# Two projection stages in one block, with handed-on weight space and split rows kept in DRAM

## What is computed

```
h = rmsnorm(x, norm_mix_pre)
z = h @ w_in                                   # 1024 -> 3584 columns
rq, rk, rv, rg, dq, dk, dv = jnp.split(z, cuts, axis=-1)     # 7 x 512 columns
rq, rk = rope(rq), rope(rk) * RET_DK ** -0.5
ro, new_ret_state = retention_scan(ret_state, rq, rk, rv, block_len)   # 4 heads, chunk by chunk
ret_out = silu(rg) * rms_normalize(ro, NORM_EPS)
dq, dk = rope(dq), rope(dk)
do = diff_attention_core(dq, k_all, v_all, mask, lam, diff_subln, lambda_init)
mix = concatenate([ret_out, diff_out]) @ w_out
x = x + rmsnorm(mix, norm_mix_post)            # then a squared-ReLU MLP in the same manner
```

## Time and profile before

| | us |
|---|---|
| median of 3 runs (lowest, highest) | 2991.37 (2988.84, 2992.09) |
| the profiled execution, device time | 2985.41 |
| its span from first to last instruction | 2983.3 |
| PE busy | 2866.2 (96%) |
| DVE, ACT, POOL busy | 1461.7 (49%), 912.0 (31%), 276.8 (9%) |
| mean granted TensorE clock, as a share of 2.4 GHz | 0.982 |

### The profile page before, as it was taken

The page is one execution under the profiler, slowest core; times in us unless marked ns, Lnnn a source line. Parts: engine busy times, 40 slices in busy tenths (PEclk is TensorE's granted clock), DMA queues, the critical chain, the costliest instruction groups (busy, mean ns, idle before and its releaser), DMA issues.

```text
span 2983.3 us, 39174 instructions
## 1 busy us (share of the span) xinstructions
PE 2866.2 (96%) x14917; PEld 2347.8 (79%) x14917; DVE 1461.7 (49%) x2971; ACT 912.0 (31%) x1870; POOL 276.8 (9%) x413
## 2 busy tenths in 40 slices
PE   6999997999978999999889999999989999999998
PEld 5888886777856777766768888888878888988987
DVE  4322333423236887777544454454475445444455
ACT  3221222322125666666422112112133221211222
POOL 1111211111112111110000000000013000000001
PEclk9999998999979999999999999999999999999999
DMA  4101102433432211110321111111123111111113
GB/s 165 35 25 36 36 22 92 145 113 112 145 112 86 82 61 57 52 35 33 110 99 54 45 42 56 42 43 56 42 94 135 43 43 42 50 49 42 42 50 123
DMA packets 105887, 204.67 MB, mean 69 GB/s; under 512 B 11248, under 2 KB 48112, under 8 KB 105776
## 3 DMA queue, kind: packets, MB, share of 16 engines
q1 hardware_dynamic: 103472, 194.79, 19.8%
q0 software_dynamic: 2304, 8.39, 0.8%
HBM read 168.28 MB, written 34.87 MB: 68 GB/s over the span
## 4 chain that ended last, share of the span: by engine, by line
PE 65%; DVE 3%; ACT 1%; DMA 1%; issue 1%; POOL 0%; POOLq 0%; SPq 0%; DVEq 0%; ACTq 0%
PE bank L2191 24%; PE bank L2229 22%; PE bank L1514 6%; PE bank L1486 4%; PE bank L1542 4%; PE bank L1527 2%; PE bank L2242 1%; PE bank L2271 1%; PE bank L1461 0%; DVE mix_S L1377 0%; DVE mix_S L1350 0%; PE bank L1497 0%; POOL mix_head_stats L1198 0%; PE bank L2182 0%; DMA mix_V<-in_w_out_dram 0%
## 5 line engine op out<-in xcount | busy, mean ns | idle before, releaser
L2191 PE MATMUL bank<-ffn_hTh,ffn_uph 128*128 128x352 f32 (+1 forms) x1280 | 452.8, 354 | 6.9 <-DVE ffn_upl L1976 5.5
L2191 PE MATMUL bank<-ffn_hTl,ffn_uph 128*128 128x352 f32 (+1 forms) x1280 | 449.4, 351 | 0.0
L2191 PE MATMUL bank<-ffn_hTh,ffn_upl 128*128 128x352 f32 (+1 forms) x1280 | 449.1, 351 | 0.0
L2058 DVE TENSOR_TENSOR ffn_facc<-bank,ffn_facc 128x512 f32<-128x512 f32 x464 | 313.7, 688 | 217.3 <-PE bank L2229 205.3
L2229 PE MATMUL bank<-ffn_dnh,ffn_hidh 128*128 128x512 f32 x960 | 380.9, 397 | 2.7 <-DVE ffn_dnl L1983 2.7
L2229 PE MATMUL bank<-ffn_dnh,ffn_hidl 128*128 128x512 f32 x960 | 379.1, 395 | 0.0
L2229 PE MATMUL bank<-ffn_dnl,ffn_hidh 128*128 128x512 f32 x960 | 378.3, 394 | 0.0
L2031 DVE SCALAR_TENSOR_TENSOR ffn_relu<-bank,ffn_relu 128x352 f32<-128x352 f32 (+1 forms) x160 | 94.6, 591 | 501.0 <-ACT ffn_relu L1875 500.9
L2191 PEld LDWEIGHTS bank<-ffn_hTh,ffn_uph 128*128 128x128 f32 x1280 | 241.2, 188 | 43.4 <-issue 18.4
L2191 PEld LDWEIGHTS bank<-ffn_hTl,ffn_uph 128*128 128x128 f32 x1280 | 241.4, 189 | 23.0
L2191 PEld LDWEIGHTS bank<-ffn_hTh,ffn_upl 128*128 128x128 f32 x1280 | 240.9, 188 | 22.6
(11 more groups left out here) (218 smaller groups left out, 4500.1 us busy)
## 6 DMA issues: line engine op xcount, KB each, us to landing
ffn_raw<-in_w_up_dram SPq DMA_DIRECT2D x64, 512.0 KB, 4.2
ffn_raw<-in_w_down_dram SPq DMA_DIRECT2D x64, 512.0 KB, 4.0
ffn_x<-x_scratch SPq DMA_DIRECT2D x21, 512.0 KB, 6.0
retp_x<-in_x_prompt_dram SPq DMA_DIRECT2D x16, 512.0 KB, 3.6
retw_raw<-in_w_in_dram SPq DMA_DIRECT2D x16, 512.0 KB, 5.0
dpp_x<-in_x_prompt_dram SPq DMA_DIRECT2D x16, 512.0 KB, 5.0
dp_kst<-in_cache_diff_k_dram SPq DMA_DIRECT2D x32, 256.0 KB, 2.8
mix_xr<-in_x_prompt_dram SPq DMA_DIRECT2D x16, 512.0 KB, 3.5
```

The source lines that it names most:

```text
L2058: nc.vector.tensor_tensor(out=part, in0=Dn[i % s.rd][:], in1=part, op=ALU.add).then_inc(s_add, 1)
L2191: last = nc.tensor.matmul(bank[:, 0:w], l[:, k, f * P:(f + 1) * P], r[:, k, c:c + w], start=(k == 0 and q == 0), stop=(k == 7 and q == 2))
```

## The change

Both projection stages stand in one phase and one block (`projection_phase`), so that there is no barrier between them, and each engine's list of the one runs on into that of the other. `retention_stage` has the prompt tiles and then the decode tile; `diff_projection_stage` begins with that decode tile, from the split rows that are still in place (`rows_h`, `rows_l`), with no load, no normalizing and no transposes. The other 16 split tiles are stored to DRAM by SP in the retention stage (`store_rows`, 2 x 512 KB a tile), and loaded again by POOL in the diff stage (`load_rows`), into a ring of two. ACT waits for a tile's store before it overwrites the pair (`act.wait_ge(s_rows, 32 * t2)`). `w_in` for the diff stage goes into the space of the retention weights: staged as soon as the staging buffers are free, split in the decode tile as each projection has used its columns. `gate` and `osc` get tiles of their own, where they lay in the staging buffers. `x` is normalized in place. `s_const` is cut into three semaphores, and POOL waits for `small` alone, which is asked for third and not behind 4 MB of weights.

In `retention_stage`, SP's list, POOL's wait, and what ACT and DVE do in the last tile and ahead of each split:

```diff
+        sp.dma_start(ident[:], ident_d).then_inc(s_ident, 16)
+        sp.dma_start(small[:], ret_tab[:, 4 * P:4 * P + 12]).then_inc(s_small, 16)
...
+        def store_rows(t):
+            sp.wait_ge(pre.s_lo, 2 * t + 2)
+            for i, part in enumerate((pre.hi[0], pre.lo[0])):
+                sp.dma_start(rows_scratch[i, t], part[:].rearrange("p k n -> p (k n)").bitcast(F32)).then_inc(s_rows, 16)
+
+        def ahead(t, n, u):
+
+            store_rows(t)
+            pre.load(sp, xv[t + 2], u, t + 3)
...
+        sp.wait_ge(s_ropeq, 2 * nt - 2)
+        sp.dma_start(rope[0][:], rv[nt][:, 0:192]).then_inc(s_rope[0], 16)
+        yield "last rows asked for"
+        store_rows(nt - 2)
+        store(nt - 1, 0, 0)
+        store_rows(nt - 1)
+        store(nt, 0, 1)
+        yield "last whole tile stored"
...
-                pool.wait_ge(s_const, 48)
...
+        pool.wait_ge(s_small, 16)
...
+            if last:
+                next_weights(act)
+            act.wait_ge(s_z, 4 * t + 4)
+            nc.scalar.activation(gate[:], Z[1][:], ACT.Silu).then_inc(s_g, 1)
+            if not last:
+                act.wait_ge(s_rows, 32 * t2)
+                pre.act_hi(act, 0, t2 + 1)
...
+            if dec_tile:
+                next_weights(dve)
```

In `diff_projection_stage`, SP's list (`earlier` is SP's list of the retention stage, run on to its next `yield`), POOL's loads of the rows, the first weights, and PE's tile:

```diff
+        next(earlier)
+        sp.wait_ge(before_it.wt.s_lo, len(before_it.wt.pieces))
+        wt.load(sp, wv, 2048, slice(0, 4))
+        load_rope(0)
+        load_rope(1)
...
+        next(earlier)
+        wt.load(sp, wv, 2048, slice(4, 8))
+        next(earlier)
+        wt.load(sp, wv, 2048, slice(8, None))
+        sp.wait_ge(before_it.s_z, 4 * nt + 4)
+        load_keys(0)
+        load_keys(1)
...
+        def load_rows(j):
+            u = j % 2
+            if j >= 2:
+                pool.wait_ge(s_z, 3 * (j - 2) + 3)
+            else:
+                pool.wait_ge(before_it.s_z, 4 * nt + 4)
+                pool.wait_ge(before_it.s_xn, nt + 1)
+                pool.wait_ge(before_it.s_rows, 32 * nt)
+            for i, part in enumerate((rows_h[u], rows_l[u])):
+                nc.gpsimd.dma_start(part[:].rearrange("p k n -> p (k n)"),
+                                    rows_scratch[i, j - 1]).then_inc(s_rows[u], 16)
...
+    def first_weights_hi(act):
+        act.wait_ge(before_it.s_z, 4 * nt + 1)
+        wt.act_hi(act, slice(0, 4))
...
-                    if j and j < nt:
-                        x_transpose(j + 1)
...
+            if j:
+                pe.wait_ge(s_rows[u], 32 * ((j + 1) // 2))
+            else:
+                pe.wait_ge(before_it.s_v, nt + 1)
```

More of the change, by code:

```diff
@@ L78, in __init__ @@
         self.half = sb("half", [P, 1])
-        self.hi = [sb(f"hTh{u}", [P, self.kt, P], F32R) for u in range(slots)]
-        self.lo = [sb(f"hTl{u}", [P, self.kt, P], F32R) for u in range(slots)]
+        self.hi, self.lo = rows
         self.s_x = [sem(f"x_loaded{u}") for u in range(depth)]
@@ L161, in __init__ @@
             self.stage = [None] * 2
-        self.hi = sb("whi", [P, chunks, kt, N], F32R)
-        self.lo = sb("wlo", [P, chunks, kt, N], F32R)
+        if like:
+            self.hi, self.lo = like.hi, like.lo
+        else:
+            home = [inner if inner and c == chunks - 1 else ctx for c in range(chunks)]
+            both = [[sb(f"w{n}{c}", [P, kt, N], F32R, home[c]) for n in ("hi", "lo")] for c in range(chunks)]
+            self.hi, self.lo = zip(*both)
         self.pieces = [(c, k) for c in range(chunks) for k in range(0, kt, self.deep)]
@@ L202, in project @@
                 pe.wait_ge(self.s_lo, (c * kt + k) // self.deep + 1)
-            for q, (l, r) in enumerate(parts(hT_hi, hT_lo, self.hi, self.lo)):
-                last = self.nc.tensor.matmul(out, l[:, k, :], r[:, c, k, :], start=(k == 0 and q == 0),
+            for q, (l, r) in enumerate(parts(hT_hi, hT_lo, self.hi[c], self.lo[c])):
+                last = self.nc.tensor.matmul(out, l[:, k, :], r[:, k, :], start=(k == 0 and q == 0),
                                              stop=(k == kt - 1 and q == 2))
@@ new lines, in retention_stage @@
+    rope = [sb(f"rope{u}", [P, 192]) for u in range(2)]
+    ident = keep.ident
+    decay = sb("decay", [P, 4 * P])
+    small = sb("small", [P, 12])
+    qn, kn = sb("qn", [P, N]), sb("kn", [P, N])
+    kg, vn = sb("kg", [P, N]), sb("vn", [P, N])
+    gate, osc = sb("gate", [P, N]), sb("osc", [P, N])
+    qT, kT, aT = sb("qT", [P, N]), sb("kT", [P, N]), sb("aT", [P, N])
+    ro = [sb(f"ro{u}", [P, N]) for u in range(2)]
+    state = [sb("state", [P, N]), sb("state_dec", [P, N])]
+    ssr, msr, rsr = sb("ssr", [P, 4]), sb("msr", [P, 4]), sb("rsr", [P, 4])
@@ L641, in _ @@
-                load_x(0)
-                sp.dma_start(pre.gain[:], gain.to_broadcast([P, 1024])).then_inc(pre.s_gain, 16)
-                wt.load(sp, wv, 2048, slice(0, 4))
-                load_rope(0)
-                for i, row in enumerate(lambdas):
-                    sp.dma_start(lam[:, i, :], row.to_broadcast([P, DK])).then_inc(s_const, 16)
-                sp.dma_start(subw[:], subln.to_broadcast([P, HD])).then_inc(s_const, 16)
-                load_x(1)
-                load_rope(1)
@@ L775, in _ @@
[L775 to L793 removed]
+                ret.scalar(act, dif.first_weights_hi)
@@ L1512, in quarter @@
             for k in range(k0, k0 + 4):
-                for p, (l, r) in enumerate(parts(mTh, mTl, wt.hi, wt.lo)):
-                    last = nc.tensor.matmul(Y[:], l[:, k, :], r[:, b, k, :], start=(k == 0 and p == 0),
+                for p, (l, r) in enumerate(parts(mTh, mTl, wt.hi[b], wt.lo[b])):
+                    last = nc.tensor.matmul(Y[:], l[:, k, :], r[:, k, :], start=(k == 0 and p == 0),
                                             stop=(k == 7 and p == 2))
```

1301 lines of the change are left out of this document (625 added, 676 removed).

## The result

| | before | changed |
|---|---|---|
| median, us (lowest, highest; four runs each, same chip) | 2990.46 (2988.84, 2992.09) | 2950.39 (2947.22, 2951.91) |
| ratio, 95% interval | | 0.987 (0.986 to 0.988) |
| span of the profiled execution, us | 2983.3 | 2945.4 |

What follows compares the result with a forecast made beforehand. PE was taken to bound both projection stages, with idle time at the hand-over. Gains of 10.2 (first tile), 25.1 (hand-over) and 14.5 us (diff tiles) sum to 49.8, so 2991.4 becomes 2941.5 us, 0.983; range 2935 to 2956.

Steps and rivals of the forecast that it cites:

- All three places: Where the change can bring something: the first tile, the hand-over, and the work on PE in the diff tiles.
- the forecast's own ends: Whole kernel: gain between 42.5 and 52.1 us, so a time of 2949 to 2939 us.
- Rival B: Diff tiles: the decode slots' chain is next late, a wait replaces the transposes; 14.5 us lost, 2956; 7 in 100.
- Rival C: Hand-over: last four weight pieces queue behind tile 1's rows, the clock falls; gain 16.3 us, 2950; 12 in 100.
- rival D: First tile: the wait for stored rows replaces that for constants; 2 of 10.2 us left, 2950; 10 in 100.
- its own signs: PE's waits for k and rows gone, scores near 42 us, first whole diff tile near 501, diff tiles every 19.3.
- Its sign of being wrong: Fewer than 40 us gained with no rival's sign, or anything moved behind the diff stage.
- First tile, 10.2 us: Tile 0: POOL adds k earlier, scores begin at 41.4 to 43.0 us; gain 9.4 to 11.0, middle taken.
- The tight row store: Retention tiles, last but two on SP's list: 5.5 us left for a 5.0 us landing; costs 0 to 2 us.
- Hand-over, 25.1 us: Retention to diff stage: first whole diff tile begins at 511.2 us before the first tile's gain; ends 26.5 and 23.7.
- Diff tiles, 14.5 us: 15 of the 16 whole diff tiles lose their transposes on PE, 0.97 us each.
- Rival A: Diff tiles: converting row loads come late and PE waits; whole gain eaten from 22.6 us a pair; 5 in 100.

Runs made afterwards that it cites:

- b_small: Kernel before, with only POOL's wait cut to `small` on its own semaphore, asked for behind the eighth weight piece, no rows stored: 2975.67 us, 0.996.
- after_2: The changed kernel run again, unedited, to see what of a trace belongs to the execution; this second execution took 2949.01 us.
- a_hand: Changed kernel with POOL's load of tile 1's rows held back until the ninth weight piece has been split: 2946.42 us, 0.986.
- a_all: Changed kernel with `small` behind the eighth weight piece, one row store earlier, tile 1's row load held back, `half` allocated last: 2939.13 us, 0.9835.

## Why the prediction was right, and where it was short

All three places were the right ones, and the time came within its range, 9 us above the forecast. But the forecast's own ends were 2949 and 2939 us, and 2950.39 lies past them: the range held because its high end was drawn to take in rivals B, C and D, none of which came at its price. That C and D each give 2950 is chance. Of its own signs, the wait for the diff rows went and PE was busy throughout the diff tiles, but PE still waited 1.8 us for k, the scores began at 45.08 us (42 said) and the first whole tile at 509.20 (501 said). Its sign of being wrong, fewer than 40 us with none of the rivals, is met by the two profiled executions (37.9) and just missed by the medians (40.1). By its own steps:

- **First tile, 10.2 us: right in price** (b_small, 10.2), **partly by luck, and short in the changed kernel (7.4).** The prediction called the last weight piece next late (41.4 us), gave k's path as the other end (43.0) and took the middle. In the twelve traces with the early add k's path sets the scores, and the last piece adds 0.2 us at most. The transposes on that path took 0.85 us in b_small and in the changed kernel, not 1.8: 0.9 us a group is what they took in the kernel before (43.89 to 44.80 us), where the clock was granted at 0.53 from 38 to 49 us. At this clock the fourth projection took 6.9 us there, 5.8 in the changed kernel at 1.00, so some 1.2 us of the gain are the clock's. The step that failed is the rope of k at 33.6 us: it was read from one trace, and ends at 33.5 to 36.4 us over 14. In the changed kernel k came 2.7 us later than in b_small, 1.4 of it by the later start of DVE, the rest by the landing of the first 12 pieces. From DVE's start to the scores it takes 45.4 us before and 36.3 after, a gain of 9.0. The price of the row store of tile 0, zero, was right: ACT waited for PE when it split tile 1, not for the store (rival D did not happen).
- **The tight row store, 0 to 2 us, taken as 0: mis-sized.** The place, the list of requests ahead of it and the time left were right. The landing was not 5.0 us but 8.3 us behind 2 MB of weights, and PE had not enough to do meanwhile: 2.1 us, in other traces up to 4.0. The text named that cause and then took the lower end.
- **Hand-over, 25.1 us: mis-sized.** First projection without a wait, as said; second 1.18 us late (1.6 said); the third waited for a piece that took some 7.3 us to land, for which 5.0 had been taken, and the clock then fell (0.76 from 502 to 509 us, 24 matmuls in 7.2 us). No row gave the 0.3 us put down for DVE's rope, and PE has no such wait: the first whole tile follows at once. Rival C named this mechanism, with 9 us for its price; a third of it came true (3.1 us). The tell it gave, a wait of over 4 us, was missed by 0.05 us here and met in after_2 (4.04 us).
- **Diff tiles, 14.5 us: two things short.** The transposes were priced at 0.97 us by their own slot; taken away they are worth 0.89 (13.3 us). And the rows went to a new place, which costs 3.2 us in the matmuls themselves. The step "all on the engine that is the bound" was right, but the prediction read the durations of what stayed as fixed. A tile came every 19.6 us (19.3 said).
- **Rival A** did not happen: POOL's row loads landed in 3.7 to 6.3 us and PE never waited for one. The estimate of 15 us a pair, from the Trainium skill (SBUF — State Buffer: the rule under Who interferes with whom, the figure under A bandwidth-pool intuition that's wrong), was not borne out in this stage, in which DVE is busy 61 of 314 us. **Rival B** did not happen: no wait in 314 us.

All four misses went one way. The row store and the hand-over took a landing from an emptier stretch than the one that it stood in; the first tile took one trace's start for every trace's; the diff tiles took a step's own slot for its price, and the durations of what stayed as given.

## What to carry to other kernels

Take a transfer's landing from a stretch that is as full as the one that it will stand in, not from an idle one, and ask for first what is waited for first. Where two paths end close together, follow both to the end and take the later, not the middle. When tiles are moved or small ones added, look at where the operands of the hot matmuls lie against each other, not only at waits: a busy share of 100% hides a slower engine. Price a removed step by taking it away, since what follows it may have been prepared in its shadow.

## What was not expected

**Placement.** A float32r matmul of 512 columns whose rows (the 128x128 operand) lie 32 bytes past a multiple of 64, with its weights at a multiple, takes 6.4 ns more than the 227 that it takes where both lie alike (2.8%). The reverse, weights off and rows in place, is not shown, nor any other type or size.

**POOL and DVE side by side.** In tile 0 of the changed kernel the add of k took 2.18 us beside DVE's low parts, and three of these took 5.41 us in a row. The same add took 1.29 us at 476.76 us in the kernel before, where DVE was idle, and a low part with no add beside it takes 1.22. Before the change the add of tile 0 met DVE's scaling and was as slow (2.23 us), so some 0.9 us stand on k's path in both kernels. No run takes the two apart, so the cause is read from these times and not shown.

**The end of the program is not as fixed as it looks.** The mix and MLP stage, the same in all kernels here, took 2120.9 to 2128.0 us. A stretch of 64 us that begins 36 us behind the last projection matmul of the diff stage, in the changed kernel and in a_hand:

```profile
858.74:922.74 64.00, 55.50 (x296) 41.72 (x295) 45.10 (x160) 37.49 (x113) 14.93 (x37) 0.99 0.29 94
```

```profile
853.64:917.64 64.00, 55.98 (x277) 42.17 (x276) 42.76 (x154) 34.23 (x104) 14.15 (x35) 0.91 0.25 83
```

In a_hand the granted clock goes to half twice more behind waits of 2 to 3 us that every kernel has there, and 64 x (0.99 - 0.91) = 5.1 us are gone, all that a_hand had gained by then: its diff stage ended 5.1 us before that of the changed kernel (817.64 and 822.74), and its span is 2945.6 us. The first trace of a_all had 0.91 too, its second 0.99 and its third 0.95, so it belongs to the execution at least in part; but the three traces of the changed kernel had 0.97 to 0.99, and what decides it stays open.
